# Five units of chunk 0 ahead at the mixer's entrance, and GpSimd centering three row blocks in the last normalization

## The chip, the cores and the metric

The kernel runs on one core of one Trainium2 chip. The metric is the device time of one execution in microseconds (us), the median of repeated runs. The engines are named as in the profile: PE is TensorE, PEld its weight loads, DVE VectorE, ACT ScalarE, POOL GpSimd, SP SyncE. Every engine works through its own instructions in order and waits on semaphores.

## What is computed

One decoder layer in float32, for 512 prompt tokens and 32 sample tokens (8 requests of 4), D_MODEL 1024, D_FF 2816:

```
h1 = LN1(ALPHA*x  + 0.5*SwiGLU_1(x))
h2 = LN2(ALPHA*h1 + Mixer(h1))
y  = LN3(ALPHA*h2 + 0.5*SwiGLU_2(h2))
LN(x) = (x - mean) * rsqrt(var + EPS) * g + b          (per token, over 1024 features)
Mixer: z = h1 @ w_in  ->  pool channels | q | k | v | two gates
       A = pooled windows 2/4/8/16 -> group map, scale, w_pool_out
       B = sliding-window attention with rotary positions and sinks -> w_attn_out
       Mixer = (sigmoid(gate_A)*A + sigmoid(gate_B)*B) @ w_out
```

## The kernel before

Activations lie with the features on the 128 partitions: 8 row blocks (KD) by 544 tokens, in two chunks c of C = 272 tokens. A *unit* is one weight tile of 1024 x 128, multiplied with one chunk. To keep float32 accuracy each operand is split into a rounded high half and a low remainder, and a product is three matmuls, so a unit of 8 row blocks is 24 matmuls of 128x272 for each chunk. Weights come by DMA from SP into four `raw` slots; `split(u)` stands in two programs: ACT copies the raw tile into the high half (L755, counted in `hi_done`), DVE subtracts it from the raw tile to get the low half (L1067, `lo_done`). In `part`, PE waits for `lo_done >= u + 1` before unit u.

`home(u)` says where a split unit lies: a ring of SLOTS = 4 places, `ring(u % SLOTS)`, but for some units elsewhere. A ring place is free when chunk 1, which runs behind chunk 0, has used the unit before it: `split` on ACT waits for `mm_done[1] >= u - (SLOTS - 1)`.

The mixer's projection has 42 units (MIX1, from MIX_BASE). All engines walk over steps s = 0, 1, ... in an order that is written out: `epilogue(s, 0)` empties PSUM after unit s of chunk 0, `epilogue(s - LAG, 1)` after unit s - 2 of chunk 1, and then comes `split(MIX_BASE + s + 2)`. PSUM banks are 2c + u % 2, so unit u of a chunk waits until unit u - 2 is emptied; unit 1 of chunk 1 waits until unit 0 of chunk 1 is. On PE the order at the entrance is: units 0 to 3 of chunk 0 (the statistics matmuls of chunk 1 after the first), then units 0 and 1 of chunk 1, then unit 4 of chunk 0, unit 2 of chunk 1, unit 5 of chunk 0, and so on by turns. ACT empties the first four units (`line`, L951) and unit 4 (`vT`, L960).

Chunk 1 is still being normalized (LN1) when the mixer begins. That work stands at steps 0 and 1: on DVE, all at s == 0, `norm_var`, `norm_center` (L1248), the split of unit 3, `norm_reciprocal` (L1253), `norm_ratio` (L1262), `norm_low` (L1270 and L1272, four pairs of row blocks into `act_hi` and `act_lo`); on ACT `norm_std` at s == 0 and eight affines (`norm_both`, L810) at s == 1. Unit 0 of chunk 1 on PE waits for `act_lo` pair by pair (`act_ready`). At s == 3 ACT makes four copies of cached pool rows (L1030), after which POOL forms the window sums (`wins`, L703).

`near_w` is a place for weights at the start of the memory in which the mixer later keeps `m1`; before the change it serves only the second FFN.

The last normalization (l = 2) of chunk 1 comes after PE's last matmul. DVE takes the variance (`norm_var`, L1238 to L1240), centers all eight row blocks with the mean in PSUM (`norm_center`, two instructions of 4 blocks, L1248), takes the reciprocal of ACT's square root (L1253), scales in four pairs (`norm_scale`, L1282), and affines blocks 5 to 7 (L1574) while ACT affines 0 to 4 (L817); SP stores four parts of y.

Of the kernel before, what the change touches and what calls it, by code (L numbers as in the profile page):

```python
# [27 lines left out]
P = 128  # L28
D = 1024
KD = D // P  # L30
# [4 lines left out]
C = T // 2  # L35
# [22 lines left out]
SLOTS = 4  # L58
RAWS = 4
HK = KD // 2  # L60
LAST_AFFINE = 5
LAG = 2
DOWN = KD
MIX1 = 42
# [11 lines left out]
MIX_BASE = FFN_UNITS  # L76
# [207 lines left out]
def program(nc, a, out):  # L284
    ctx = ExitStack()
    with ctx:
# [3 lines left out]
        def sem(name):  # L290
            return ctx.enter_context(nc.semaphore(name))
# [124 lines left out]
        var_done = [sem(f"var_done{c}") for c in range(2)]  # L416
        std_done = [sem(f"std_done{c}") for c in range(2)]
        center_done = [sem(f"center_done{c}") for c in range(2)]
        rec_done = [sem(f"rec_done{c}") for c in range(2)]
        norm_done = [sem(f"norm_done{c}") for c in range(2)]  # L420
        low_hi = [sem(f"low_hi{c}") for c in range(2)]
# [23 lines left out]
        def tok(c):  # L445
            return slice(c * C, c * C + C)
# [28 lines left out]
        def stat_bank(l, c):  # L475

            return 6 if c else 4
# [5 lines left out]
        def ring(s):  # L483

            return ring_hi[:, s], ring_lo[:, s]

        def home(u):

            down = is_down(u)
            if down:  # L490
                li, g, i = down
                if g < len(GROUPS_F) - 1 or i < 2:
                    return ring(((0 if li else 2) + i) % SLOTS)
                if i < SLOTS:
                    w = (x_w, s_w)[i - 2]
                    return w[:, 0], w[:, 1]
                flat = t_op[:, i - SLOTS].rearrange("p h k t -> p h (k t)")
                return tuple(flat[:, h, 0:D].rearrange("p (k n) -> p k n", k=KD) for h in range(2))
            if FFN2_BASE <= u < FFN2_BASE + 2:
                i = u - FFN2_BASE  # L500
                return near_w[:, 2 * i], near_w[:, 2 * i + 1]
            if FFN2_BASE - SLOTS <= u < FFN2_BASE:
                return spare[u - (FFN2_BASE - SLOTS)]
            return ring(u % SLOTS)

        def op_home(li, i):
# [211 lines left out]
            all_norm_sums(2)  # L718


        @block.scalar
        def _(act):

            def split(u):

                n = load_of(u)
                act.wait_ge(raw_in[n % RAWS], loaded(n))
                down = is_down(u)
                if down and down[1] == len(GROUPS_F) - 1:
                    li, _, i = down  # L730

                    act.wait_ge(op_lo, PRODS * li + (PRODS if i == 3 else 0))
                    act.wait_ge(prod_mm, PRODS * (li + 1) if i >= SLOTS else PRODS * li + PRODS - 2 * SLOTS + 2 * i + 2)
                elif down and down[2] < SLOTS:
                    li, g, i = down
                    act.wait_ge(prod_mm, PRODS * li + 7 * FIRST_PAIR[g + 1] - 2 * SLOTS + 2 * i + 2)
                elif MIX_BASE <= u < MIX_BASE + 2:

                    act.wait_ge(prod_mm, PRODS)
                elif MIX_BASE + 2 <= u < MIX_BASE + SLOTS:  # L740

                    act.wait_ge(mm_done[1], MIX_BASE - DOWN + u - MIX_BASE - 1)
                elif FFN2_BASE - SLOTS <= u < FFN2_BASE:
                    act.wait_ge(mm_done[1], WO_BASE)
                elif FFN2_BASE <= u < FFN2_BASE + 2:
                    act.wait_ge(m_done[1], KD)
                    act.wait_ge(mm_done[1], WO_BASE)
                elif FFN2_BASE + 2 <= u < FFN2_BASE + PLAIN:

                    act.wait_ge(mm_done[1], u - (2 * SLOTS - 1))  # L750
                elif u >= SLOTS:

                    act.wait_ge(mm_done[1], u - (SLOTS - 1))
                kn = unit_kind(u)
                act.activation(home(u)[0][:, 0:kn, :], raw[:, n % RAWS, 0:kn, :], ACT.Copy).then_inc(hi_done, 1)  # L755
# [42 lines left out]
            def norm_std(l, c):  # L798
                act.wait_ge(var_done[c], l + 1)
                act.activation(stat[:, c, :], stat[:, c, :], ACT.Sqrt, bias=mean_w[:, P:P + 1]) \  # L800
                    .then_inc(std_done[c], 1)
# [209 lines left out]
            def beside(at):  # L1011
                for name in STAGES.get(at, []):
                    if name == "vkout" or name in GROUPS or name[0] == "T":
                        att_copies(name)
                if at in EXP_AT:
                    exps(EXP_AT.index(at))

            for s in range(MIX1 + LAG):
                if s < MIX1:
                    epilogue(s, 0)  # L1020
                if s == 0:
                    norm_std(0, 1)
                if s == 1:
                    norm_both(0, 1)
                if s == 3:
                    act.wait_ge(mixer_in, 16 * MIXER_DMAS)
                    segs = line[:, :, BUF + SEQ:LINE].rearrange("p g (b s) -> p g b s", s=SEG)
                    rows = uctx.rearrange("p (g b s) -> p g b s", g=NG, b=DB)
                    for g in range(NG):
                        act.activation(segs[:, g, :, 0:BUF], rows[:, g], ACT.Copy).then_inc(uctx_done, 1)  # L1030
                beside(s - 0.5)
                if s >= LAG:
                    epilogue(s - LAG, 1)
                    split(MIX_BASE + s + 2)
                beside(s)
            split(WO_BASE + 4)
# [7 lines left out]
                    norm_both(1, 0, *WO_AFFINE[s, c])  # L1044
            ffn(2, DOWN)

            norm_std(2, 1)
            norm_affine(1)

# [2 lines left out]
        def _(dve):  # L1052
# [3 lines left out]
            def step(ins):  # L1056

                ins.then_inc(v_step, 1)
                steps[0] += 1
                dve.wait_ge(v_step, steps[0])  # L1060
# [171 lines left out]
            def norm_var(l, c):  # L1232

                dve.wait_ge(stats_done[c], l + 1)
                bank = stat_bank(l, c)
                s = stat[:, c, :]

                step(dve.tensor_tensor(s, psum[:, bank, 0:C], s, ALU.subtract))  # L1238
                step(dve.tensor_tensor(s, s, s, ALU.mult))
                dve.tensor_tensor(s, psum[:, bank ^ 1, 0:C], s, ALU.subtract).then_inc(var_done[c], 1)  # L1240

            def norm_center(l, c):

                bank = stat_bank(l, c)
                mean = psum[:, bank:bank + 1, 0:C].broadcast_to([P, 4, C])
                for i in range(2):
                    half = y[:, 4 * i:4 * i + 4, tok(c)]
                    ins = dve.tensor_tensor(half, half, mean, ALU.subtract)  # L1248
                ins.then_inc(center_done[c], 1)
# [25 lines left out]
            def norm_scale(c, lo=0, hi=KD):  # L1275

                dve.wait_ge(center_done[c], 3)
                dve.wait_ge(rec_done[c], 3)
                r = stat[:, c:c + 1, :].broadcast_to([P, 2, C])
                for i in range(lo // 2, hi // 2):  # L1280
                    pair = y[:, 2 * i:2 * i + 2, tok(c)]
                    dve.tensor_tensor(pair, pair, r, ALU.mult).then_inc(norm_done[c], 1)  # L1282

# [238 lines left out]
            def beside(at):  # L1522
                for name in STAGES.get(at, []):
                    if name in GROUPS:
                        grouped(name)
                    elif name[0] == "S":
                        scores(name)
                    elif name[0:2] == "PV":
                        attended(name)
                for g in POOLED_AT.get(at, ()):  # L1530
                    pooled(g)
                if at in DIVIDE_AT:
                    divide(DIVIDE_AT.index(at))

            for s in range(MIX1 + LAG):
                if s < MIX1:
                    epilogue(s, 0)
                if s == 0:
                    norm_var(0, 1)
                    norm_center(0, 1)  # L1540
                    split(MIX_BASE + 3)
                    norm_reciprocal(0, 1)
                    norm_ratio(0, 1)
                    norm_low(0, 1)
                beside(s - 0.5)
                if s >= LAG:
                    epilogue(s - LAG, 1)
                    split(MIX_BASE + s + 2)
                beside(s)
            split(WO_BASE + 4)  # L1550
# [27 lines left out]
        def _(pe):  # L1578
# [280 lines left out]
            for s in range(MIX1 + LAG):  # L1859
                if s < MIX1:  # L1860
                    mix_part(s, 0)
                if s == 0:
                    stats(0, 1)
                beside(s - 0.5)

                for m in (0, 1) if s == LAG + 1 else (s - LAG,) if s > LAG else ():
                    mix_part(m, 1)
                beside(s)
            def m_wait(c):
# [115 lines left out]
```

## Time and profile before

| | us |
|---|---|
| median of 3 runs (lowest, highest) | 1074.93 (1074.66, 1077.04) |
| the profiled execution's own time | 1075.05 |
| its span, first to last instruction | 1072.8 |
| PE busy in it | 1046.1 |
| DVE busy | 808.3 |
| ACT busy | 479.7 |
| POOL busy | 102.7 |

The profile is of one execution. Times in a timeline count from the start of its span. A row's duration is that of one instruction, or of all of them where several are merged (x4); matmuls overlap, so a matmul row of 0.29 us does not mean that the next begins 0.29 us later. In brackets stands how long the engine was idle before the row, and the line that released it.

### The profile page before, as it was taken

Reading aid. Unit: us, or ns where it says so; the run is one execution under the profiler, and the core shown is the slowest. Engines: PE = TensorE matmul, PEld = TensorE weight load, DVE = VectorE, ACT = ScalarE, POOL = GpSimd, SP = SyncE. Lnnn points to the kernel's source line nnn. Section 1 sums busy time; section 2 is a strip of 40 time slices with the busy share of each in tenths; the row PEclk is TensorE's granted clock in tenths of the full one; section 3 lists DMA queues with packets and bytes.
Section 4 is the critical chain, followed back from the end, with each engine's and each line's share of the span. In section 5 each row is a group of like instructions: output and inputs, shape, how many; then the busy total and the mean of one; then the engine's idle time right before and its main releaser. Section 6 shows DMA issues by size and latency. Waiting matters only on the chain.

```text
span 1072.8 us, 20782 instructions
## 1 busy us (share of the span) xinstructions
PE 1046.1 (98%) x8197; PEld 1028.9 (96%) x8197; DVE 808.3 (75%) x1313; ACT 479.7 (45%) x846; POOL 102.7 (10%) x110
## 2 busy tenths in 40 slices
PE   8999999999999989999999999989999999999995
PEld 8999999999999989998799999979999999999994
DVE  7994999549997776976545576898589963799765
ACT  6543555225554442475632253545355531455433
POOL 2000000000003335000000024200000000000043
PEclk9999999999999999999999999989999999999998
DMA  9333423313234132211122250113322232232302
GB/s 328 107 104 110 139 87 109 108 60 119 79 119 150 47 121 99 69 60 31 59 90 86 96 188 26 40 60 94 104 99 98 100 119 79 79 111 87 118 1 84
DMA packets 60064, 103.69 MB, mean 97 GB/s; under 512 B 6649, under 2 KB 19257, under 8 KB 59945
## 3 DMA queue, kind: packets, MB, share of 16 engines
q1 hardware_dynamic: 58656, 97.94, 27.3%
q0 software_dynamic: 1312, 4.44, 1.2%
q8 instruction: 66, 1.08, 0.4%
q14 instruction: 30, 0.24, 0.1%
HBM read 99.86 MB, written 3.68 MB: 97 GB/s over the span
## 4 chain that ended last, share of the span: by engine, by line
PE 84%; DVE 8%; issue 3%; ACT 2%; POOL 1%; DMA 1%; SPq 1%; DVEq 0%; POOLq 0%; ACTq 0%
PE psum L1595 14%; PE psum L1597 14%; PE psum L1596 14%; PE psum L1669 13%; PE psum L1670 13%; PE psum L1671 13%; DVE y L1248 1%; DVE ring_lo L1074 1%; POOL p L662 1%; DVE t_op L1122 1%; DMA raw<-in_ffn_up 1%; DVE t L1117 1%; DVE stat L1253 1%; PE psum L1802 1%; DVE act_lo L1272 1%
## 5 line engine op out<-in xcount | busy, mean ns | idle before, releaser
L1669 PE MATMUL psum<-t_op,ring_hi 128*128 128x272 f32 x640 | 185.4, 290 | 5.3 <-DVE ring_lo L1074 2.7
L1671 PE MATMUL psum<-t_op,ring_lo 128*128 128x272 f32 x640 | 185.7, 290 | 0.0
L1670 PE MATMUL psum<-t_op,ring_hi 128*128 128x272 f32 x640 | 185.1, 289 | 0.0
L1067 DVE TENSOR_TENSOR ring_lo<-raw,ring_hi 128x1024 fp32r<-128x1024 f32 (+2 forms) x87 | 97.1, 1117 | 99.0 <-ACT ring_hi L755 98.9
L1595 PE MATMUL psum<-act_hi,ring_hi 128*128 128x272 f32 x512 | 149.5, 292 | 6.0 <-DVE act_lo L1272 2.4
L1597 PE MATMUL psum<-act_hi,ring_lo 128*128 128x272 f32 x512 | 147.7, 289 | 0.0
L1595 PE MATMUL psum<-hid,ring_hi 128*128 128x272 f32 x512 | 147.4, 288 | 0.0
L1596 PE MATMUL psum<-act_lo,ring_hi 128*128 128x272 f32 x512 | 147.4, 288 | 0.0
L1596 PE MATMUL psum<-hid,ring_hi 128*128 128x272 f32 x512 | 147.0, 287 | 0.0
L1597 PE MATMUL psum<-hid,ring_lo 128*128 128x272 f32 x512 | 146.7, 287 | 0.0
L775 ACT ACTIVATE ring_hi<-sums 128x512 fp32r<-128x512 f32 x160 | 99.8, 629 | 103.7 <-PE psum L1671 68.4
L1669 PE MATMUL psum<-act_hi,ring_hi 128*128 128x272 f32 x480 | 139.1, 290 | 0.0
L1670 PE MATMUL psum<-act_lo,ring_hi 128*128 128x272 f32 x480 | 138.8, 289 | 0.0
L1671 PE MATMUL psum<-act_hi,ring_lo 128*128 128x272 f32 x480 | 138.3, 288 | 0.0
L755 ACT ACTIVATE ring_hi<-raw 128x1024 fp32r<-128x1024 f32 (+2 forms) x87 | 81.5, 938 | 112.3 <-PE psum L1597 96.7
L1669 PEld LDWEIGHTS psum<-t_op,ring_hi 128*128 128x128 f32 x640 | 121.3, 190 | 6.2 <-issue 5.8
L1670 PEld LDWEIGHTS psum<-t_op,ring_hi 128*128 128x128 f32 x640 | 121.6, 190 | 0.0
L1671 PEld LDWEIGHTS psum<-t_op,ring_lo 128*128 128x128 f32 x640 | 121.4, 190 | 0.0
L1074 DVE TENSOR_TENSOR ring_lo<-sums,ring_hi 128x512 fp32r<-128x512 f32 x160 | 106.8, 684 | 4.9 <-ACT ring_hi L775 4.7
L1595 PEld LDWEIGHTS psum<-act_hi,ring_hi 128*128 128x128 f32 x512 | 96.4, 188 | 10.5 <-issue 5.8
L1597 PEld LDWEIGHTS psum<-hid,ring_lo 128*128 128x128 f32 x512 | 96.4, 188 | 0.0
L1596 PEld LDWEIGHTS psum<-act_lo,ring_hi 128*128 128x128 f32 x512 | 96.4, 188 | 0.0
(247 smaller groups left out, 2447.1 us busy)
## 6 DMA issues: line engine op xcount, KB each, us to landing
raw<-in_ffn_up SPq DMA_DIRECT2D x175, 256.0 KB, 2.9
raw<-in_ffn_down SPq DMA_DIRECT2D x64, 256.0 KB, 2.9
raw<-in_mix_wide SPq DMA_DIRECT2D x52, 256.0 KB, 2.9
raw<-in_ffn_down SPq DMA_DIRECT2D x32, 192.0 KB, 2.4
raw<-in_mix_proj SPq DMA_DIRECT2D x32, 128.0 KB, 2.2
raw<-in_w_out SPq DMA_DIRECT2D x16, 256.0 KB, 2.8
y<-in_x SPq DMA_DIRECT2D x2, 1088.0 KB, 12.7
xin<-in_x SPq DMA_DIRECT2D x3, 544.0 KB, 6.7
```

Source lines behind the costliest of these rows:

```text
L662: pool.tensor_tensor(total, total, sq[:, sq_slot(c, k), :], ALU.add).then_inc(sqsum_done[c], 1)
L755: act.activation(home(u)[0][:, 0:kn, :], raw[:, n % RAWS, 0:kn, :], ACT.Copy).then_inc(hi_done, 1)
L775: act.activation(op_home(li, i)[0], op_source(li, i), ACT.Copy).then_inc(op_hi, 1)
L1067: dve.tensor_tensor(lo[:, 0:kn, :], raw[:, n % RAWS, 0:kn, :], hi[:, 0:kn, :], ALU.subtract) \
L1074: dve.tensor_tensor(lo, op_source(li, i), hi, ALU.subtract).then_inc(op_lo, 1)
L1117: dve.tensor_tensor(terms[i], first, second, ALU.subtract).then_inc(term_sum, 1)
L1595: pe.matmul(o, w[0][:, k, :], x(k, 0), start=k == 0, stop=False)
L1596: pe.matmul(o, w[0][:, k, :], x(k, 1), start=False, stop=False)
L1597: ins = pe.matmul(o, w[1][:, k, :], x(k, 0), start=False, stop=k == kn - 1)
L1669: pe.matmul(o, w[0][:, k, :], x[0], start=k == 0, stop=False)
L1670: pe.matmul(o, w[0][:, k, :], x[1], start=False, stop=False)
L1671: ins = pe.matmul(o, w[1][:, k, :], x[0], start=False, stop=k == HK - 1)
```

## The change

At the mixer's entrance, PE takes unit 4 of chunk 0 ahead of unit 0 of chunk 1, and then units 0, 1 and 2 of chunk 1 in a row. The ring has no free place for a fifth unit, so unit 4 lies in `near_w`; its split waits for the last matmul of the first FFN instead of for unit 0 of chunk 1, and is moved, on ACT and on DVE, ahead of `epilogue(0, 1)` in step s == 2.

In the last normalization of chunk 1, DVE centers row blocks 0 to 4 in one instruction. ACT copies the mean from PSUM into `tmp_a` once DVE's first subtract has read it, and POOL centers blocks 5 to 7 with that copy. DVE waits for the copy before it centers, and for POOL before it scales blocks 4 to 7.

```
@@ -59,6 +59,7 @@
 RAWS = 4
 HK = KD // 2
 LAST_AFFINE = 5
+MINE = 5
 LAG = 2
 DOWN = KD
 MIX1 = 42
@@ -416,6 +417,9 @@
         var_done = [sem(f"var_done{c}") for c in range(2)]
         std_done = [sem(f"std_done{c}") for c in range(2)]
         center_done = [sem(f"center_done{c}") for c in range(2)]
+        mean_read = sem("mean_read")
+        mean_out = sem("mean_out")
+        end_centered = sem("end_centered")
         rec_done = [sem(f"rec_done{c}") for c in range(2)]
         norm_done = [sem(f"norm_done{c}") for c in range(2)]
         low_hi = [sem(f"low_hi{c}") for c in range(2)]
@@ -501,6 +505,8 @@
                 return near_w[:, 2 * i], near_w[:, 2 * i + 1]
             if FFN2_BASE - SLOTS <= u < FFN2_BASE:
                 return spare[u - (FFN2_BASE - SLOTS)]
+            if u == MIX_BASE + SLOTS:
+                return near_w[:, 0], near_w[:, 1]
             return ring(u % SLOTS)
 
         def op_home(li, i):
@@ -718,6 +724,12 @@
             all_norm_sums(2)
 
 
+            pool.wait_ge(mean_out, 1)
+            rest = y[:, MINE:KD, tok(1)]
+            pool.tensor_tensor(rest, rest, tmp_a[:, 1:2, :].broadcast_to([P, KD - MINE, C]), ALU.subtract) \
+                .then_inc(end_centered, 1)
+
+
         @block.scalar
         def _(act):
 
@@ -740,6 +752,8 @@
                 elif MIX_BASE + 2 <= u < MIX_BASE + SLOTS:
 
                     act.wait_ge(mm_done[1], MIX_BASE - DOWN + u - MIX_BASE - 1)
+                elif u == MIX_BASE + SLOTS:
+                    act.wait_ge(mm_done[1], MIX_BASE)
                 elif FFN2_BASE - SLOTS <= u < FFN2_BASE:
                     act.wait_ge(mm_done[1], WO_BASE)
                 elif FFN2_BASE <= u < FFN2_BASE + 2:
@@ -1029,8 +1043,11 @@
                     for g in range(NG):
                         act.activation(segs[:, g, :, 0:BUF], rows[:, g], ACT.Copy).then_inc(uctx_done, 1)
                 beside(s - 0.5)
+                if s == LAG:
+                    split(MIX_BASE + SLOTS)
                 if s >= LAG:
                     epilogue(s - LAG, 1)
+                if s > LAG:
                     split(MIX_BASE + s + 2)
                 beside(s)
             split(WO_BASE + 4)
@@ -1044,6 +1061,8 @@
                     norm_both(1, 0, *WO_AFFINE[s, c])
             ffn(2, DOWN)
 
+            act.wait_ge(mean_read, 1)
+            act.activation(tmp_a[:, 1, :], psum[:, stat_bank(2, 1), 0:C], ACT.Copy).then_inc(mean_out, 1)
             norm_std(2, 1)
             norm_affine(1)
 
@@ -1235,13 +1254,24 @@
                 bank = stat_bank(l, c)
                 s = stat[:, c, :]
 
-                step(dve.tensor_tensor(s, psum[:, bank, 0:C], s, ALU.subtract))
+                ins = dve.tensor_tensor(s, psum[:, bank, 0:C], s, ALU.subtract)
+                if (l, c) == (2, 1):
+                    ins.then_inc(mean_read, 1)
+                    dve.wait_ge(mean_read, 1)
+                else:
+                    step(ins)
                 step(dve.tensor_tensor(s, s, s, ALU.mult))
                 dve.tensor_tensor(s, psum[:, bank ^ 1, 0:C], s, ALU.subtract).then_inc(var_done[c], 1)
 
             def norm_center(l, c):
 
                 bank = stat_bank(l, c)
+                if (l, c) == (2, 1):
+                    dve.wait_ge(mean_out, 1)
+                    mine = y[:, 0:MINE, tok(c)]
+                    dve.tensor_tensor(mine, mine, psum[:, bank:bank + 1, 0:C].broadcast_to([P, MINE, C]),
+                                      ALU.subtract).then_inc(center_done[c], 1)
+                    return
                 mean = psum[:, bank:bank + 1, 0:C].broadcast_to([P, 4, C])
                 for i in range(2):
                     half = y[:, 4 * i:4 * i + 4, tok(c)]
@@ -1278,6 +1308,8 @@
                 dve.wait_ge(rec_done[c], 3)
                 r = stat[:, c:c + 1, :].broadcast_to([P, 2, C])
                 for i in range(lo // 2, hi // 2):
+                    if c and 2 * i + 2 > MINE:
+                        dve.wait_ge(end_centered, 1)
                     pair = y[:, 2 * i:2 * i + 2, tok(c)]
                     dve.tensor_tensor(pair, pair, r, ALU.mult).then_inc(norm_done[c], 1)
 
@@ -1543,8 +1575,11 @@
                     norm_ratio(0, 1)
                     norm_low(0, 1)
                 beside(s - 0.5)
+                if s == LAG:
+                    split(MIX_BASE + SLOTS)
                 if s >= LAG:
                     epilogue(s - LAG, 1)
+                if s > LAG:
                     split(MIX_BASE + s + 2)
                 beside(s)
             split(WO_BASE + 4)
@@ -1863,7 +1898,7 @@
                     stats(0, 1)
                 beside(s - 0.5)
 
-                for m in (0, 1) if s == LAG + 1 else (s - LAG,) if s > LAG else ():
+                for m in (0, 1, 2) if s == LAG + 2 else (s - LAG,) if s > LAG + 2 else ():
                     mix_part(m, 1)
                 beside(s)
             def m_wait(c):
```

## Rows read from the trace of the kernel before

**Rows 1.** The page's summary: span, then busy time, share and instructions of TensorE.

```profile
span 1072.8 us, 20782 instructions
...
PE 1046.1 (98%) x8197; PEld 1028.9 (96%) x8197; DVE 808.3 (75%) x1313; ACT 479.7 (45%) x846; POOL 102.7 (10%) x110
```

**Rows 2.** TensorE's waits, whole span: total us, times, longest us.

```profile
PE psum L1595 <- DVE act_lo L1272: 2.4, 3, 2.0
...
PE psum L1787 <- DVE att_lo L1519: 0.8, 1, 0.8
```

**Rows 3.** TensorE's timeline, 391 to 411: start us, us, engine, line, operation [idle before].

```profile
393.48 0.28 PE L1597 MATMUL psum<-act_hi,ring_lo 128*128 128x272 f32 x1
395.81 0.36 PE L1595 MATMUL psum<-act_hi,ring_hi 128*128 128x272 f32 x1 [2.05 <-DVE act_lo L1272]
...
400.00 0.28 PE L1597 MATMUL psum<-act_hi,ring_lo 128*128 128x272 f32 x1
401.03 0.36 PE L1595 MATMUL psum<-act_hi,ring_hi 128*128 128x272 f32 x1 [0.74 <-ACT u_new L955]
...
410.13 0.29 PE L1595 MATMUL psum<-act_hi,ring_hi 128*128 128x272 f32 x1
```

**Rows 4.** ScalarE's timeline, 370 to 412, same columns.

```profile
392.88 4.15 ACT L810 ACTIVATE y<-y,vecs 128x272 f32<-128x272 f32 x8 [4.71 <-DVE y L1262]
396.94 0.38 ACT L951 ACTIVATE line<-psum 128x272 f32<-128x272 f32 x1
...
401.98 0.90 ACT L1030 ACTIVATE line<-p 128x120 f32<-128x120 f32 x4
404.31 0.37 ACT L951 ACTIVATE line<-psum 128x240 f32<-128x240 f32 x1 [1.43 <-PE psum L1597]
...
404.74 1.07 ACT L755 ACTIVATE ring_hi<-raw 128x1024 fp32r<-128x1024 f32 x1
```

**Rows 5.** VectorE's timeline, 380 to 450.

```profile
398.49 0.72 DVE L1272 TENSOR_TENSOR act_lo<-y,act_hi 128x544 fp32r<-128x544 f32 x1
401.86 1.23 DVE L1067 TENSOR_TENSOR ring_lo<-raw,ring_hi 128x1024 fp32r<-128x1024 f32 x1 [2.65 <-ACT ring_hi L755]
405.84 2.29 DVE L1067 TENSOR_TENSOR ring_lo<-raw,ring_hi 128x1024 fp32r<-128x1024 f32 x1 [2.76 <-ACT ring_hi L755]
...
413.48 0.42 DVE L1394 TENSOR_TENSOR p<-psum,cos_sin 128x272 f32<-128x272 f32 x1
```

**Rows 6.** GpSimd's timeline, 403 to 450.

```profile
402.96 1.31 POOL L703 TENSOR_TENSOR wins<-line 128x678 f32<-128x678 f32 x1 [17.44 <-ACT line L1030]
404.35 5.25 POOL L703 TENSOR_TENSOR wins<-wins 128x676 f32<-128x676 f32 x3
...
411.16 3.56 POOL L703 TENSOR_TENSOR wins<-wins 128x676 f32<-128x676 f32 x2
```

**Rows 7.** TensorE's timeline, 704 to 724.

```profile
708.76 0.36 PE L1669 MATMUL psum<-t_op,ring_hi 128*128 128x272 f32 x1 [1.29 <-issue]
...
713.23 0.57 PE L1669 MATMUL psum<-t_op,ring_hi 128*128 128x272 f32 x1 [2.73 <-DVE ring_lo L1074]
```

**Rows 8.** Windows: length, busy us by engine (instructions), granted clock, DMA share, GB/s.

```profile
711.00:712.50 1.50, 0.00 (x0) 0.00 (x0) 1.50 (x3) 1.50 (x5) 0.00 (x0) 1.00 0.57 191
...
713.20:717.30 4.10, 3.06 (x12) 2.77 (x12) 4.03 (x8) 1.75 (x3) 0.00 (x0) 0.50 0.39 136
717.30:722.70 5.40, 5.34 (x23) 5.38 (x24) 5.40 (x10) 0.63 (x1) 0.00 (x0) 0.50 0.11 38
```

**Rows 9.** VectorE's timeline, 1056 to the end.

```profile
1060.05 0.44 DVE L1238 TENSOR_TENSOR stat<-psum,stat 128x272 f32<-128x272 f32 x1 [1.28 <-PE psum L1705]
...
1061.36 2.47 DVE L1248 TENSOR_TENSOR y<-y,psum 128x1088 f32<-128x1088 f32 x2
1063.75 1.84 DVE L1253 RECIPROCAL stat<-stat 128x272 f32<-128x272 f32 x1
1065.70 2.63 DVE L1282 TENSOR_TENSOR y<-y,stat 128x544 f32<-128x544 f32 x4
```

More of the change, by code:

```diff
@@ L61 @@
 LAST_AFFINE = 5
+MINE = 5
 LAG = 2
@@ L418, in program @@
         center_done = [sem(f"center_done{c}") for c in range(2)]
+        mean_read = sem("mean_read")
+        mean_out = sem("mean_out")
+        end_centered = sem("end_centered")
         rec_done = [sem(f"rec_done{c}") for c in range(2)]
@@ L503, in home @@
                 return spare[u - (FFN2_BASE - SLOTS)]
+            if u == MIX_BASE + SLOTS:
+                return near_w[:, 0], near_w[:, 1]
             return ring(u % SLOTS)
@@ L718, in _ @@
             all_norm_sums(2)
+            pool.wait_ge(mean_out, 1)
+            rest = y[:, MINE:KD, tok(1)]
+            pool.tensor_tensor(rest, rest, tmp_a[:, 1:2, :].broadcast_to([P, KD - MINE, C]), ALU.subtract) \
+                .then_inc(end_centered, 1)
         @block.scalar
@@ L742, in split @@
                     act.wait_ge(mm_done[1], MIX_BASE - DOWN + u - MIX_BASE - 1)
+                elif u == MIX_BASE + SLOTS:
+                    act.wait_ge(mm_done[1], MIX_BASE)
                 elif FFN2_BASE - SLOTS <= u < FFN2_BASE:
@@ L1031, in _ @@
                 beside(s - 0.5)
+                if s == LAG:
+                    split(MIX_BASE + SLOTS)
                 if s >= LAG:
                     epilogue(s - LAG, 1)
+                if s > LAG:
                     split(MIX_BASE + s + 2)
@@ L1045, in _ @@
             ffn(2, DOWN)
+            act.wait_ge(mean_read, 1)
+            act.activation(tmp_a[:, 1, :], psum[:, stat_bank(2, 1), 0:C], ACT.Copy).then_inc(mean_out, 1)
             norm_std(2, 1)
@@ L1236, in norm_var @@
                 s = stat[:, c, :]
-                step(dve.tensor_tensor(s, psum[:, bank, 0:C], s, ALU.subtract))
+                ins = dve.tensor_tensor(s, psum[:, bank, 0:C], s, ALU.subtract)
+                if (l, c) == (2, 1):
+                    ins.then_inc(mean_read, 1)
+                    dve.wait_ge(mean_read, 1)
+                else:
+                    step(ins)
                 step(dve.tensor_tensor(s, s, s, ALU.mult))
@@ L1244, in norm_center @@
                 bank = stat_bank(l, c)
+                if (l, c) == (2, 1):
+                    dve.wait_ge(mean_out, 1)
+                    mine = y[:, 0:MINE, tok(c)]
+                    dve.tensor_tensor(mine, mine, psum[:, bank:bank + 1, 0:C].broadcast_to([P, MINE, C]),
+                                      ALU.subtract).then_inc(center_done[c], 1)
+                    return
                 mean = psum[:, bank:bank + 1, 0:C].broadcast_to([P, 4, C])
@@ L1280, in norm_scale @@
                 for i in range(lo // 2, hi // 2):
+                    if c and 2 * i + 2 > MINE:
+                        dve.wait_ge(end_centered, 1)
                     pair = y[:, 2 * i:2 * i + 2, tok(c)]
@@ L1545, in _ @@
                 beside(s - 0.5)
+                if s == LAG:
+                    split(MIX_BASE + SLOTS)
                 if s >= LAG:
                     epilogue(s - LAG, 1)
+                if s > LAG:
                     split(MIX_BASE + s + 2)
@@ L1864, in _ @@
                 beside(s - 0.5)
-                for m in (0, 1) if s == LAG + 1 else (s - LAG,) if s > LAG else ():
+                for m in (0, 1, 2) if s == LAG + 2 else (s - LAG,) if s > LAG + 2 else ():
                     mix_part(m, 1)
```

## The prediction

> **What bounds the kernel now.** First the page's summary: the profiled span is 1072.8 us and TensorE (PE) is busy for 1046.1 of it, 98% [rows 1]. So an edit pays only where it removes PE idle time, or time after PE's last matmul; on another engine it costs only where PE comes to wait for it. Second, the waits of PE over the whole span: one of the longest is 2.0 us, of 2.4 in three, on the normalized activations of chunk 1 (`act_lo`) [rows 2], and it lies where the change acts. Third, PE's own timeline there. The last matmul of unit 3, chunk 0, starts at 393.48, so PE could go on at 393.60; unit 0 of chunk 1 starts at 395.81, drags (its last matmul starts at 400.00 instead of 2.9 us after its first, because `act_lo` comes pair by pair), and unit 1 of chunk 1 starts only at 401.03, after ScalarE (ACT) has evacuated unit 0 [rows 3]. From 401.03 to 410.13, where unit 5 of chunk 0 begins, three units run without a gap: 9.10 / 3 = 3.03 us for a unit of 24 matmuls, 0.126 us each. From 393.60 to 410.13 PE has 16.53 us for four units (0, 1 and 2 of chunk 1, 4 of chunk 0), 12.1 us of work: 4.4 us are idle. That is all the entrance can give.
>
> **Part 1, the entrance.** PE's new order is units 0 to 4 of chunk 0, then 0, 1, 2 of chunk 1, then 5 of chunk 0. Nothing is added to PE's work; unit 4 moves ahead of three units. The question is when unit 4 can start, since everything behind it on PE now waits for it. It needs three things.
>
> Its bank: unit 2 of chunk 0 must be evacuated. ACT does that at 396.94, straight behind the eight affines of chunk 1 (392.88 to 397.0), and is done at 397.3 [rows 4]. That alone is too late for 393.60.
>
> Its high half: the ACT copy of unit 4 stands, after the change, right behind that evacuation instead of behind unit 0 of chunk 1. It takes 1.07 [rows 4]: 397.3 to 398.3.
>
> Its low half: the subtract on VectorE (DVE). In DVE's program the moved split stands at s == 2, and the whole normalization of chunk 1, `norm_low` included, stands at s == 0. So the subtract is queued behind the last `act_lo` of chunk 1, which starts at 398.49 and takes 0.72: free at 399.2 [rows 5]. The subtract takes 1.23 where GpSimd (POOL) is quiet [rows 5], as it is until 402.96 [rows 6]: done at 400.4, and PE follows a DVE release about 0.15 us later: unit 4 starts at 400.55.
>
> So the unit that is to cover the normalization waits for weights that DVE makes only after that normalization. PE stands idle from 393.60 to 400.55, 6.95 us, while the data of unit 0 of chunk 1 are there piece by piece from 395.8. Behind it unit 0 of chunk 1 runs with no drag; the wait for its evacuation (1.03 us from its last matmul's start to unit 1's first, less the usual 0.13: 0.9) stays, as unit 1's bank rule is untouched.
>
> Then unit 5. Its split waits, as before, for unit 1 of chunk 1, whose slot it takes. Before the change two units of PE work (4 and 2) lay between; now only unit 2 does. From the start of unit 1: its evacuation begins 3.28 later (401.03 to 404.31), unit 5's ACT copy 0.43 after that (404.74) and lasts 1.07, so DVE begins 4.8 after unit 1's start [rows 3, 4]. The subtract took 2.29 there, since POOL's window sums ran beside it from 404.35 [rows 5, 6]. After the change those sums wait for ACT to evacuate unit 0 of chunk 1, which also lets unit 1 start, then unit 3 of chunk 0 (0.4), then to make four context copies (0.90 [rows 4]): they begin about 1.2 us into unit 1, and their first group alone lasts 6.6 us [rows 6], so the subtract meets them again. Ready: 4.8 + 2.3 + 0.15 = 7.25 after unit 1's start; PE is free after two units, 6.05. A new wait of 1.2 us; with the quiet subtract of 1.23 it is 0.1. I take 1.2, as POOL's work lies in the same place.
>
> Idle after the change: 6.95 + 0.9 + 1.2 = 9.05 us against 4.4: **+4.6 us** (3.5 to 4.9). SP's loads do not bind: unit 4's raw weights were landed long before, and the loads behind them are released by earlier subtracts, not later ones. From unit 5 on the order of all queues is as before.
>
> **The clock.** Idle time has a second price. In the second FFN PE stood still for 1.29 us (to 708.76) and 2.73 us (to 713.23) [rows 7]; the granted clock was 1.00 until 712.5, then 0.50, that is 1.2 instead of 2.4 GHz, until 722.7 [rows 8]. After the gap of 2.05 us at the entrance it stayed at 1.00 [rows 2, 3]. A gap of 6.95 us is longer than any of these, so I expect the fall. Price, from the stretch in which PE ran on without a gap until the clock came back: 23 matmuls took 5.34 us where 23 x 0.126 = 2.9 would do: **+2.4 us**. Bounds: 0 if it does not fall, and with the 12 matmuls in 3.06 us of the stretch before it (1.5 more) 4.0.
> The Trainium skill, "TensorE: Matmul & The Clock Gate" (What's actually happening), says that the low level is the default, that sustained matmul work releases it and that an idle array falls back to it. By that rule unit 4 starts at the low level and the sum has the clock's term; the 2.05 us gap, which the clock survived, is the row that speaks against applying it to every gap, and without it the sum is 2.4 us less. The fall at 712.5 agrees with the rule.
>
> **Part 2, the end.** After PE's last matmul DVE alone sets the end: two centerings of 4 x 272 (1061.36, 2.47 together), the reciprocal (1063.75, 1.84), four scalings (1065.70, 2.63) [rows 9], and three affines whose results the last stores take. One centering of 5 x 272 replaces two of 4 x 272: at 2.47 / 2176 per element 1360 cost 1.54: **-0.9 us**. What is added must stay under cover. ACT's copy of the mean (0.38 for such a PSUM row [rows 4]) starts after DVE's first subtract of the mean (1060.05, 0.44 [rows 9]); it is done near 1061.0, before the centering's 1061.4. ACT's square root comes 0.5 us later than the copy and the centering hides it. POOL's centering of 816 elements: 678 take 1.31 [rows 6], so 1.6 us, from 1061.0 to 1062.6, some 3 us before the third scaling asks for it. The cover is gone only if POOL takes 5 us. Does POOL slow DVE? Beside POOL a subtract of two SBUF operands went from 1.23 to 2.29, but a product of 272 with a PSUM operand took 0.42 in POOL's 411.16 to 414.7 [rows 5, 6], no more than the subtract of 272 with a PSUM operand that had POOL quiet (0.44 [rows 9]); the centering reads PSUM, and the two-operand scalings begin after POOL is done. Bounds -0.9 and, if the centering lost 1.1 us to POOL all the same, +0.2.
>
> **Sum.** +4.6 + 2.4 - 0.9 = +6.1 us on the profiled execution's 1075.05 (span 1072.8): 1081.15. The median of the three runs is 0.12 lower: **1081.0 us**, 0.57% slower. What a measurement tells from no change here is about 0.2%, 2.15 us.
>
> **Rivals.**
> 1. *The clock holds.* For: it held after 2.05 us. Against: it fell after 2.73. 4.6 - 0.9 = +3.7: 1078.6.
> 2. *The fifth unit does cover the normalization* (the other side). Then U4 runs from 393.60 to 396.6, and unit 0 of chunk 1 follows with some 0.5 us of drag on the last pair; idle 0.5 + 0.9 + 1.2 = 2.6 against 4.4, -1.8, with the end -2.7: 1072.2. It decides on one time: when unit 4's low half is done. At 400.4 it costs 4.6; the entrance and the end together break even at about 396.9, which needs the subtract to run before the last two `act_lo` pairs. Against: DVE's order is written out, and it does not.
> 3. *The second FFN keeps its clock.* Shifted by some microseconds, the two short gaps at 707 to 713 may no longer bring the fall: -4.0 at most on top of the sum, +2.1: 1077.0. For: the fall came late in the second gap (712.5 of 713.2). Against: neither gap changes.
> 4. *Only the end counts*: unit 4's wait is given back later where other engines set the pace. Against: PE has no idle left to absorb it; between 410 and 700 the longest wait is 0.8 us [rows 2], and what it waits for is fed by PE itself. About 1075, within 0.2%.
>
> **How the numbers follow.** Forecast (clock falls) 0.72, rival 1 0.12, rival 3 0.07, rival 2 0.04, rival 4 and what I have not seen 0.05. The range takes rival 1, the bounds of the clock's term and of unit 5's wait: 2.4 to 8.8 us over the median, 1077.3 to 1083.7. Rival 3 and part of 4 lie at or inside 0.2%: same 0.07; faster 0.05; slower 0.88.
>
> **What would show it.** Right: on PE one wait of about 7 us ahead of the fifth unit, released by DVE's `ring_lo` subtract (now writing `near_w`), and no wait on `act_lo`; a granted clock of 0.5 behind it for some 5 us; the DVE subtract right behind the last `act_lo`; a wait of about 1 us ahead of unit 5; one DVE centering of 128x1360 of about 1.5 us, POOL's of 128x816 done before the scalings. Wrong: unit 4 starting before 397, the clock at 1.00 throughout, or DVE's third scaling waiting for POOL.

## The result, and the profile after

The changed kernel takes 1080.15 us (median of 7 runs) where the kernel before takes 1075.14 (7 runs): ratio 1.004, 95% interval 1.0031 to 1.0049 (the two medians alone give 1.0047). It is slower by 5.0 us; the forecast was 1081.0, 6.1 over the median that it started from, with 1077.3 to 1083.7 as its range. The profiled execution took 1080.8 us, its span is 1078.8.

The waits of TensorE over the whole span of the changed kernel (total us, times, longest) answer to [rows 2]:

```profile
PE psum L1630 <- DVE near_w L1086: 6.6, 1, 6.6
...
PE psum L1630 <- ACT u_new L969: 0.7, 1, 0.7
```

The 2.4 us on `act_lo` at the entrance are gone. In their place stands one wait of 6.6 us, released by VectorE's (DVE's) subtract into `near_w`: unit 4's low half. PE's timeline there, against [rows 3]:

```profile
394.99 0.28 PE L1632 MATMUL psum<-act_hi,ring_lo 128*128 128x272 f32 x1
...
401.91 0.59 PE L1630 MATMUL psum<-act_hi,near_w 128*128 128x272 f32 x1 [6.64 <-DVE near_w L1086]
...
407.52 0.37 PE L1630 MATMUL psum<-act_hi,ring_hi 128*128 128x272 f32 x1
...
411.51 0.36 PE L1630 MATMUL psum<-act_hi,ring_hi 128*128 128x272 f32 x1 [0.74 <-ACT u_new L969]
...
417.73 0.39 PE L1630 MATMUL psum<-act_hi,ring_hi 128*128 128x272 f32 x1
```

Unit 3 of chunk 0 ends at 395.11 (a matmul after 394.99), unit 5 begins at 417.73: 22.6 us, where before it was 16.5 (393.60 to 410.13). The whole stretch lies 1.5 us later than before, which comes from the first 50 us of the execution and not from the change (last section). Unit 4 takes 5.61 us (401.91 to 407.52) instead of 3.03. The windows say why (length, busy us by engine, and third from the end the granted clock):

```profile
395.10:399.00 3.90, 0.17 (x2) 0.00 (x0) 3.23 (x7) 3.90 (x9) 0.00 (x0) 0.80 0.01 5
399.00:401.90 2.90, 0.00 (x0) 0.00 (x0) 2.75 (x4) 0.77 (x1) 0.00 (x0) 0.50 0.00 0
401.90:407.50 5.60, 5.59 (x24) 5.59 (x25) 0.00 (x0) 0.00 (x0) 0.00 (x0) 0.50 0.27 94
407.50:410.50 3.00, 3.00 (x25) 3.00 (x24) 0.00 (x0) 0.00 (x0) 0.00 (x0) 0.97 0.00 0
```

The clock fell from 2.4 to 1.2 GHz while PE stood idle and came back as unit 4 ended. VectorE's timeline shows the queue, and at the end of the kernel the new centering, which answers to [rows 9]; the last two rows are GpSimd's (POOL's), the window sum that unit 5's split meets and the new centering:

```profile
400.00 0.73 DVE L1302 TENSOR_TENSOR act_lo<-y,act_hi 128x544 fp32r<-128x544 f32 x1
400.64 1.22 DVE L1086 TENSOR_TENSOR near_w<-raw,near_w 128x1024 fp32r<-128x1024 f32 x1
416.32 1.35 DVE L1086 TENSOR_TENSOR ring_lo<-raw,ring_hi 128x1024 fp32r<-128x1024 f32 x1 [14.46 <-ACT ring_hi L769]
...
1066.91 0.44 DVE L1257 TENSOR_TENSOR stat<-psum,stat 128x272 f32<-128x272 f32 x1 [1.28 <-PE psum L1740]
...
1068.22 1.56 DVE L1272 TENSOR_TENSOR y<-y,psum 128x1360 f32<-128x1360 f32 x1
1069.69 1.85 DVE L1283 RECIPROCAL stat<-stat 128x272 f32<-128x272 f32 x1
1071.64 2.63 DVE L1314 TENSOR_TENSOR y<-y,stat 128x544 f32<-128x544 f32 x4
```
```profile
415.28 1.31 POOL L709 TENSOR_TENSOR wins<-wins 128x672 f32<-128x672 f32 x1
...
1067.86 1.91 POOL L729 TENSOR_TENSOR y<-y,tmp_a 128x816 f32<-128x816 f32 x1 [3.86 <-ACT tmp_a L1065]
```

The subtract for unit 4 stands right behind the last `act_lo` of chunk 1. At the end, from DVE's first subtract of the mean to its first scaling it is 4.73 us (1066.91 to 1071.64) against 5.65 before: 0.92 less. POOL is done at 1069.8, before the scalings.

### The profile page after: what moved, and what is told of

It reads as the page before. It is cut to its first block, busy times and chain, and to the rows that moved or that the text cites. A ratio compares the mean times of both kernels' runs of the same rounds, so it can differ in the third digit from the quotient of the medians.

```text
span 1078.8 us, 20783 instructions
## 1 busy us (share of the span) xinstructions
PE 1047.7 (97%) x8197; PEld 1030.9 (96%) x8197; DVE 806.1 (75%) x1312; ACT 479.7 (44%) x847; POOL 105.5 (10%) x111
## 4 chain that ended last, share of the span: by engine, by line
PE 87%; DVE 6%; issue 2%; ACT 2%; POOL 1%; DMA 1%; SPq 0%; DVEq 0%; POOLq 0%; ACTq 0%
PE psum L1630 15%; PE psum L1632 15%; PE psum L1631 15%; PE psum L1704 13%; PE psum L1705 13%; PE psum L1706 13%; POOL p L668 1%; DVE stat L1283 1%; PE psum L1837 1%; DVE y L1278 1%; DVE act_lo L1302 1%; PE psum L1853 1%; DVE y L1292 1%; DMA xin<-in_x 1%; PE psum L1870 0%
## 5 line engine op out<-in xcount | busy, mean ns | idle before, releaser
L1086 DVE TENSOR_TENSOR ring_lo<-raw,ring_hi 128x1024 fp32r<-128x1024 f32 (+2 forms) x86 | 94.6, 1100 | 106.0 <-ACT ring_hi L769 105.9
L1630 PE MATMUL psum<-act_hi,ring_hi 128*128 128x272 f32 x496 | 145.4, 293 | 4.3 <-DVE ring_lo L1324 2.1
L1632 PE MATMUL psum<-act_hi,ring_lo 128*128 128x272 f32 x496 | 143.8, 290 | 0.0
L1631 PE MATMUL psum<-act_lo,ring_hi 128*128 128x272 f32 x496 | 143.5, 289 | 0.0
L1704 PE MATMUL psum<-act_hi,ring_hi 128*128 128x272 f32 x480 | 138.7, 289 | 0.0
L1705 PE MATMUL psum<-act_lo,ring_hi 128*128 128x272 f32 x480 | 138.4, 288 | 0.0
L1706 PE MATMUL psum<-act_hi,ring_lo 128*128 128x272 f32 x480 | 137.9, 287 | 0.0
L1630 PEld LDWEIGHTS psum<-hid,ring_hi 128*128 128x128 f32 x512 | 96.3, 188 | 0.1
```

The costliest lines, as they stand in the source:

```text
L1086: dve.tensor_tensor(lo[:, 0:kn, :], raw[:, n % RAWS, 0:kn, :], hi[:, 0:kn, :], ALU.subtract) \
L1630: pe.matmul(o, w[0][:, k, :], x(k, 0), start=k == 0, stop=False)
L1631: pe.matmul(o, w[0][:, k, :], x(k, 1), start=False, stop=False)
L1632: ins = pe.matmul(o, w[1][:, k, :], x(k, 0), start=False, stop=k == kn - 1)
L1704: pe.matmul(o, w[0][:, k, :], x[0], start=k == 0, stop=False)
L1705: pe.matmul(o, w[0][:, k, :], x[1], start=False, stop=False)
```

## The experiments

Each ratio is to the kernel before, run on the same chip. The entrance is measured in each profile from the end of unit 3 to the start of unit 5 of chunk 0 on PE: 16.5 us before, 22.6 after.

**One part alone.** `e_entrance` is the changed kernel with the last normalization as before, `e_end` the kernel before with the new last normalization.

> The entrance part alone, the last normalization as before. My theory: the entrance costs 6.1 us in the changed kernel's trace (16.53 us from unit 3's end to unit 5's start before, 22.62 after), and the last normalization gives 0.9 back, so this kernel takes 0.9 us more than the changed one: about 1081.0 us where before takes 1075.1, ratio 1.0055. Rival: the end is set by the stores and gives nothing; then it takes what the changed kernel takes, 1080.2, ratio 1.0047.

> The last normalization alone, the entrance as before. My theory: VectorE's chain at the end is 0.9 us shorter (one centering of 1.56 us in place of 2.47 us) and nothing else moves: about 1074.2 us, ratio 0.9992, hardly to be told from 1; the trace must show 0.9 us less between VectorE's first subtract of the mean and its last affine. Rival: GpSimd's centering or the wait for the copied mean eats it: ratio 1.000, and the trace shows the scaling late.

Measured: the entrance alone 1081.18 us, ratio 1.0055 (1.0043 to 1.0067); the end alone 1073.92, ratio 0.9988 (0.9979 to 0.9997). The whole loss is the entrance's. In the trace of `e_end` the first subtract stands at 1061.80 and the first scaling at 1066.53, 4.73 us, the same 0.92 less than before; in that of `e_entrance` 1066.32 and 1071.97, 5.65. Neither POOL nor the copied mean takes anything back.

**What idle costs by the clock.** `e_fill` gives PE work in the gap:

```
+ if s == LAG + 2:
+     for _ in range(14):
+         pe.matmul(psum[:, 5, 0:C], mean_w[:, 0:P], fsum[:, 1, :], start=True, stop=True)
  mix_part(s, 0)
```

> The changed kernel with 14 matmuls of 128x272 in full float32 (0.46 us each, 6.4 us in all) into a free PSUM bank, right ahead of unit 4 of chunk 0, where TensorE otherwise stands idle for 6.6 us. Their results are not used. My theory (idle costs twice, the second time by the clock): the granted clock stays at 1.00, unit 4 takes 3.0 instead of 5.6 us, and the time falls by 2.5 us to about 1077.6, ratio 1.0023. Rival: the slow unit 4 has another cause (its weights' place): no gain, 1080.2, ratio 1.0047, and unit 4 still takes 5.6 us.

Measured: 1078.94 us, ratio 1.0033 (1.0021 to 1.0044). Windows of its trace, the filled gap and unit 4:

```profile
395.90:402.60 6.70, 6.50 (x29) 5.06 (x27) 5.91 (x10) 4.59 (x9) 0.00 (x0) 1.00 0.00 1
402.60:405.70 3.10, 3.07 (x24) 3.07 (x25) 0.00 (x0) 0.00 (x0) 0.00 (x0) 1.00 0.52 169
```

Unit 4 starts 6.8 us behind unit 3's end, as in the changed kernel, waiting for `near_w` for the last 0.23 us, but at full clock: 3.1 us instead of 5.6. The entrance takes 20.05 us, 2.56 less than in the changed kernel. So of the 6.1 us in the changed kernel's profile, 2.6 are the clock and 3.5 the wait. The ratio's interval holds the 1.0023 that was expected, at its edge, and leaves out 1.0047. But it overlaps that of the changed kernel, and the two medians (1080.15 and 1078.94) lie 1.2 us apart, half of what the trace shows. The profiled executions agree with the trace: the span is 1.9 us shorter (1076.9) although unit 3 ended 0.7 us later (395.83 against 395.11).

**Is the lead at fault, or the late split?** `e_early` keeps the lead and moves the split of unit 4 (abridged; on ACT the split's wait is also loosened, from the last matmul of the first FFN to an earlier unit of it):

```
 ACT   split(MIX_BASE + 3)
+      split(MIX_BASE + SLOTS)          (and no longer at s == LAG)
-      act.wait_ge(mm_done[1], MIX_BASE)
+      act.wait_ge(mm_done[1], MIX_BASE - DOWN + SLOTS + 1)
 DVE   if s == 0:
+          split(MIX_BASE + 3); split(MIX_BASE + SLOTS)
           norm_var(0, 1); norm_center(0, 1)
-          split(MIX_BASE + 3)
```

> The changed kernel with the split of unit 4 made early: on ScalarE right behind the split of unit 3, on VectorE the splits of units 3 and 4 both ahead of chunk 1's variance, where VectorE is idle. The lead of five units stays. My theory (unit 4's low half came too late, not the lead itself): unit 4 starts right behind unit 3, no wait of 6.6 us and no fall of the clock at the entrance, unit 0 of chunk 1 loses about 0.3 us; idle there 0.3 + 0.9 + 0.1 to 1.2 against 4.4 before, and 0.9 off the end: about 1071.5 us, ratio 0.9966. Rival: the lead itself costs (later evacuations of chunk 1, window sums later): the time stays near 1080, ratio 1.004.

Measured: 1077.32 us, ratio 1.0016 (1.0005 to 1.0026). A miss: better than the change, not better than before. The longest entry among PE's waits, and ScalarE's (ACT's) timeline behind it:

```profile
PE psum L1628 <- ACT line L966: 3.5, 1, 3.5
```
```profile
393.76 4.15 ACT L824 ACTIVATE y<-y,vecs 128x272 f32<-128x272 f32 x8 [4.49 <-DVE y L1291]
397.82 0.38 ACT L966 ACTIVATE line<-psum 128x272 f32<-128x272 f32 x1
```

With the low half early, unit 4 waited for its other need, its bank: ACT evacuates unit 2 of chunk 0 only behind the eight affines of chunk 1. There were two holds, and the one that ends earlier had stayed. In this profile the clock stayed at 1.00 through the 3.48 us, and the entrance took 16.8 us. The 12 runs fall into two groups: five at 1075.16 to 1075.58 with mean clocks of 0.990 to 0.993, of which the profile is one, and seven at 1077.2 to 1079.25 with 0.986 to 0.988. A fall of the clock behind the gap in the seven would account for it, but no profile here shows one. The next two kernels take the second hold away, alone and together with the first (abridged; `e_cover` has the edit of `e_early` too):

```
-ACT   if s < MIX1: epilogue(s, 0)
+      if s < MIX1 and s != LAG: epilogue(s, 0)
       ...
       if s == 1:
+          epilogue(LAG, 0)
           norm_both(0, 1)
```

> The changed kernel with one step of ScalarE moved: the evacuation of unit 2, chunk 0, stands ahead of chunk 1's eight affines instead of behind them; unit 4's split stays where the change put it. The theory now: unit 4 is held by two things, its bank (free at 398.3 to 398.8 behind the affines) and its low half (done some 3 us later); here only the earlier one goes. So nothing changes: unit 4 starts where it did, some 6.6 us idle, ratio 1.0047. Rival: the bank is the whole hold, and the low half follows it closely; then unit 4 starts up to 3 us earlier, ratio 1.002 or less.

> The changed kernel with both holds gone: the early split of units 3 and 4 (as in the run before) and the early evacuation of unit 2 of chunk 0. The theory: unit 4 starts right behind unit 3, unit 0 of chunk 1 runs without a drag, and from unit 3's end to unit 5's start TensorE needs 13.2 us against 16.5 before the change: -3.3, with the end -4.2, and the clock does not fall at the entrance: about 1070.9 us where before takes 1075.1, ratio 0.996. Rival: a third hold appears, or the lead has a cost of its own: ratio 0.999 to 1.0016.

Measured: `e_evac` 1080.09 us, ratio 1.004 (1.0026 to 1.0054); `e_cover` 1070.39, ratio 0.9952 (0.994 to 0.9965). Alone, the early evacuation changes nothing: PE still waits 6.64 us for `near_w`. With both holds gone PE's timeline has no wait ahead of unit 4:

```profile
394.78 0.28 PE L1631 MATMUL psum<-act_hi,ring_lo 128*128 128x272 f32 x1
394.91 0.29 PE L1629 MATMUL psum<-act_hi,near_w 128*128 128x272 f32 x1
...
408.04 0.39 PE L1629 MATMUL psum<-act_hi,ring_hi 128*128 128x272 f32 x1
```

From 394.91 to 408.04 it is 13.1 us (13.2 expected, 16.5 before), and the granted clock is 1.00 over the whole of 375 to 425. The lead shows no cost of its own; this kernel beats both.

**The gap ahead of unit 1 of chunk 1.** `e_cover_bank` also loosens that unit's bank rule (`pe.wait_ge(evac[1], u - 1)` instead of `u`).

> The same with one more wait loosened: unit 1 of chunk 1 waits for the evacuation of the last unit of the first FFN, not for that of unit 0 of chunk 1, whose bank it does not use. The theory: the gap of 0.74 us ahead of unit 1 of chunk 1 goes, 0.9 us less than the kernel without this: about 1070.0, ratio 0.9953. Rival: unit 5's split, which waits for unit 1, then comes no earlier and takes the gap back as a wait ahead of unit 5: ratio as without it.

Measured: 1070.7 us, ratio 0.9958 (0.9946 to 0.9971), the same as without it. The gap of 0.74 us is gone and one of 0.96 stands ahead of unit 5, on its `ring_lo`: the rival was right. Unit 1 ends earlier, but the split behind it meets a window sum and takes 2.33 us instead of 1.34.

**What decides the length of unit 5's split.** `e_phase` puts a memset on POOL ahead of the window sums:

```
  pool.wait_ge(uctx_done, NG)
+ pool.memset(wins[:, 1, :], 0.0).then_inc(win_step, 1)
- steps = 1
+ steps = 2
```

> The changed kernel with one memset on GpSimd ahead of its window sums, which shifts them by some 0.6 to 0.8 us against VectorE's split of unit 5. The theory (a two-operand subtract of VectorE and a GpSimd sum run one after the other, whichever began first): a sum is then under way when the split begins, the split lasts as much longer as the sums came later (1.35 to about 2.0 us), and the wait ahead of unit 5 grows from 0.14 to about 0.8 us; time +0.6, ratio about 1.005. Rival (both merely slow each other): the split stays near 1.35 us, or doubles whatever the phase.

Measured: 1080.77 us, ratio 1.0049 (1.0035 to 1.0062). POOL, DVE and PE in its trace:

```profile
411.35 0.67 POOL L694 MEMSET wins<- 128x679 f32 x1 [24.21 <-ACT line L1045]
412.20 1.31 POOL L710 TENSOR_TENSOR wins<-line 128x678 f32<-128x678 f32 x1 [0.18 <-POOL wins L694]
413.59 1.32 POOL L710 TENSOR_TENSOR wins<-wins 128x676 f32<-128x676 f32 x1
414.98 1.31 POOL L710 TENSOR_TENSOR wins<-wins 128x672 f32<-128x672 f32 x1
416.37 2.47 POOL L710 TENSOR_TENSOR wins<-wins 128x664 f32<-128x664 f32 x1
```
```profile
415.21 2.16 DVE L1087 TENSOR_TENSOR ring_lo<-raw,ring_hi 128x1024 fp32r<-128x1024 f32 x1 [13.28 <-ACT ring_hi L770]
```
```profile
417.42 0.39 PE L1631 MATMUL psum<-act_hi,ring_hi 128*128 128x272 f32 x1 [0.79 <-DVE ring_lo L1087]
```

A sum was under way from 414.98 to 416.29 when the split was due at 415.21. The split took 2.16 and ended at 417.37, 1.1 us after that sum; PE waited 0.79 us for unit 5. The next sum, due while the split ran, took 2.47. Counted from the start of unit 1 of chunk 1 on PE, the sums began 0.82 us later than in the changed kernel (1.81 instead of 0.99), the split lasted 0.81 longer (2.16 instead of 1.35), and unit 5 started 0.80 later behind unit 2. The total moved by too little to tell: its interval overlaps that of the changed kernel. In this profile the longer wait is also hidden, since the clock came back halfway through unit 4 (0.52 granted from 401.90 to 405.20, 1.00 from there to 407.00): unit 4 took 4.48 us instead of 5.61 and the entrance 22.2. So the price of the fall is not one number. Over the 3.03 us at full clock it was 2.6 in the changed kernel and in `e_evac`, 2.35 in `e_entrance` and 1.45 here.

## Why the prediction was right, and where it was off

Unit 4 behind DVE's normalization: right, and shown. Its start, 6.8 us behind unit 3's end, was forecast as 6.95; `e_evac` and `e_cover` show that DVE's place for the split was the later of two holds.

The clock: right that it falls, which all four profiles with the gap of 6.64 us show. It was forecast at 2.4 us and `e_fill` measures 2.56; that the size fits so well is in part luck, as `e_phase` paid 1.45. The reason given also leaned on the gap of 2.05 us that the clock had survived; `e_end`, with the same gap, was followed by a fall (last section), so that row could not bound a safe gap.

Unit 5's wait: the mis-sized term. It was put at 1.2 us, because the subtract had taken 2.29 beside POOL's sums [rows 5]; PE lost some 0.15 us there (417.46 to 417.73 at 0.126 a matmul). The subtract took 1.35 (416.32 to 417.67): it met the last 0.27 us of a sum (415.28 to 416.59), where before it had met one from nearly its beginning. The step that failed is "POOL's work lies in the same place": what counts is which sum is under way at that moment. The prediction had the numbers for it: it put the sums' start at 1.2 us into unit 1, and they follow each other by 1.39 [rows 6], so the third would run from 4.0 to 5.3, with the split due at 4.8. 7.0 forecast for the entrance with the clock, less this 1.1, is 5.9; the traces say 6.1. With the end's 0.9 off that is 5.2, against the 5.0 measured between the medians. The spans of the two profiled executions differ by 6.0, of which the timelines give 5.8: 1.5 from the first 50 us, 6.1 at the entrance, 0.9 less at the end, and 0.9 less in the second FFN (below), which the forecast did not have.

The end: right at -0.9 (0.92). POOL's centering took 1.91 instead of 1.6, far under its cover.

Rival 2 had the wrong condition. "It decides on one time: when unit 4's low half is done" left out the bank, although the same text had ACT's evacuation at 397.3; `e_early` had the low half in time and still ended above the kernel before. Unit 4 needs both. Its price was too small as well: with both needs met, -2.7 came out as -5.2 (1070.39 against 1075.63). The entrance gave 3.4 (16.5 to 13.1) where 1.8 was forecast, since neither the drag of 0.5 nor the 1.2 of unit 5 came, and the end gave 0.9. The profiled spans agree (2.9 shorter, and unit 3 ended 1.3 later: 4.2), and the ratio's interval holds these 4.3. What is left to 5.2, 0.9, is not shown; executions in which the kernel before loses its clock at the entrance (last section) would be one source. Its break-even at 396.9 needs the subtract ahead of the last three `act_lo` pairs, not two: before, they started at 394.94, 396.12, 397.30 and 398.49.

Rivals 1 and 4 did not occur: the clock did not hold at the entrance, and the loss was not given back where other engines set the pace. Rival 3 occurred in part in this profile: the second FFN still lost its clock (0.50 from 723 to 727), but for a shorter time, and got it back near 728.7. PE was 7.7 us later than before ahead of it and 6.85 behind it.

The range does not come out of the bounds that it names: 3.5 + 0 - 0.9 is 2.6 and 4.9 + 4.0 - 0.9 is 8.0, where 2.4 and 8.8 are written, and the 4.9 is not worked out. The result lies inside either.

## What to carry to other kernels

Work moved forward to cover a wait covers it only if all it needs is ready without the engines that cause the wait: look up each of its releases (weights, bank) in the order of the engine that makes it, and count all of them, since freeing one only uncovers the next. An idle stretch on TensorE can cost again through the clock, here 1.5 to 2.6 us on 6.6. And when two engines take turns, a duration read beside another engine's work holds for that moment only: ask which instruction will be under way.

## What had not been expected of the hardware

A gap of one length did not always have one outcome, nor a longer gap a worse one. `e_early` kept its clock through 3.48 us in its profile. The kernel before kept its clock through 2.05 us at the entrance in its profile; in `e_end`, with the same entrance, the same gap of 2.05 us was followed by a fall in unit 0 of chunk 1 (0.70 on average):

```profile
396.00:398.10 2.10, 0.05 (x1) 0.03 (x1) 1.65 (x4) 2.10 (x5) 0.00 (x0) 1.00 0.01 4
398.10:403.80 5.70, 4.95 (x24) 4.46 (x24) 3.09 (x6) 2.18 (x8) 0.00 (x0) 0.70 0.01 3
```

And it fell in the first 20 us of some executions: 0.80 from 12 to 20 us in the changed kernel's profile, 0.71 in `e_end`'s, 1.00 in the kernel before's, after gaps of about 2 us at 11 us in all three. By the starts of the same matmuls in the two timelines, the changed kernel was 0.5 us late behind that gap (11.30 instead of 10.80), 2.0 at 16 us, of which 1.5 are the clock's, and 1.5 from 50 us to the entrance; no instruction of the change runs that early. What decides whether a gap of 2 us brings the fall was not tried and stays open.

DVE's subtract of two SBUF operands and POOL's sums ran in turn: 1.2 us with POOL quiet, 1.35 to 2.39 by the moment at which it met a sum, ending some 1.1 us after that sum (before, 405.84 to 408.13 against a sum of 405.74 to 407.05), and a sum that began during a subtract took up to 2.48 instead of 1.31. The Trainium skill, "SBUF — State Buffer" (Who interferes with whom), says that a VectorE instruction with two SBUF inputs contends with a GpSimd instruction that reads SBUF, that the port pair they share is an exclusive lock, and that issue order decides who blocks; `e_phase` agrees, with 2.16 us for the split that met the sum early.
